# A decoder layer on one core: norm2's sums of late token tiles moved one tile down, four activation splits moved to GpSimd, v transposed instead of multiplied by the identity

## The reference

```
h = rmsnorm(x, norm1_w) * (1 + sc1) + sh1 ;  p = h @ w_in
ya = rmsnorm(a_b * conv3(a_c * a_x)) ;  q, k, v = silu(conv4(qkv))
# DeltaNet, chunk by chunk, state S (128 x 128 per head):
#   v_new = u - w @ S ;  o = q_dec @ S + intra @ v_new ;  S = S * decay + k_dec.T @ v_new
y = concat([ya, rmsnorm(o) * silu(z)]) @ w_out ;  x = x + gt1 * y
h = rmsnorm(x, norm2_w) * (1 + sc2) + sh2
gate, up = split(conv3(h @ w_up)) ;  x = x + gt2 * ((silu(gate) * up) @ w_down)
return rmsnorm(x, norm_f_w)
```

## Time and profile before

| what | us |
|---|---|
| median of 3 runs | 1449.6 (1446.66 to 1451.29) |
| the profiled execution, its own time | 1450.17 |
| its span in the profile | 1447.9 |
| PE busy in the span | 1358.7 (94%) |
| DVE, ACT, POOL busy | 776.0, 554.3, 727.1 |
| mean granted PE clock | 0.966 |

### The profile page before, as it was taken

One profiled execution on the slowest core, in us unless ns is written; L12 is line 12 of the kernel. 1 busy time (PEld: TensorE's weight loads), 2 busy tenths in 40 slices (PEclk: granted clock), 3 DMA queues, 4 the chain that ended last, 5 costly groups with the idle time before them and its releaser, 6 DMA issues.

```text
span 1447.9 us, 18240 instructions
## 1 busy us (share of the span) xinstructions
PE 1358.7 (94%) x6739; PEld 1139.2 (79%) x6739; DVE 776.0 (54%) x959; ACT 554.3 (38%) x749; POOL 727.1 (50%) x488
## 2 busy tenths in 40 slices
PE   3799999999969999989986999999999999999997
PEld 3478888888858999877875888888888877888886
DVE  2834244262446666626465655565556556457544
ACT  3234535262531221215275444444444443324321
POOL 4457758686742212222067655656565565443540
PEclk8699999999969999989998999999999999999999
DMA  8152424224240000110111333322223347443611
GB/s 330 37 131 59 130 72 116 79 81 130 58 132 1 1 0 0 58 59 1 30 30 29 88 87 88 87 81 75 74 78 88 87 156 265 147 138 117 233 36 58
DMA packets 137929, 128.42 MB, mean 89 GB/s; under 512 B 7423, under 2 KB 114188, under 8 KB 137868
## 3 DMA queue, kind: packets, MB, share of 16 engines
q1 hardware_dynamic: 137868, 127.60, 29.1%
HBM read 111.85 MB, written 15.74 MB: 88 GB/s over the span
## 4 chain that ended last, share of the span: by engine, by line
PE 68%; POOL 10%; issue 9%; DVE 7%; DMA 3%; ACT 2%; SPq 0%; POOLq 0%; DVEq 0%; ACTq 0%
PE ps L1930 18%; PE ps L1931 18%; PE ps L1932 18%; PE ps L2060 5%; POOL ada_raw L814 3%; PE ps L2079 3%; PE ps L2076 3%; POOL ada_raw L817 2%; POOL w_split L789 2%; DMA ada_first<-in_ada_w_dram 1%; POOL ada_raw L819 1%; DVE ada_first L1440 1%; DVE pm_b L1584 1%; DMA x_hi<-in_x_dram 1%; POOL ada_sum L823 1%
## 5 line engine op out<-in xcount | busy, mean ns | idle before, releaser
L1930 PE MATMUL ps<-h_p,w_units 128*128 128x512 f32 x616 | 241.2, 392 | 11.7 <-POOL h_p L913 10.2
L1932 PE MATMUL ps<-h_p,w_units 128*128 128x512 f32 x616 | 240.6, 391 | 0.0
L1931 PE MATMUL ps<-h_p,w_units 128*128 128x512 f32 x616 | 240.6, 391 | 0.0
L1930 PE MATMUL ps<-h,w_split 128*128 128x512 f32 x448 | 175.6, 392 | 0.0
L1932 PE MATMUL ps<-h,w_split 128*128 128x512 f32 x448 | 175.1, 391 | 0.0
L1931 PE MATMUL ps<-h,w_split 128*128 128x512 f32 x448 | 175.0, 391 | 0.0
L924 POOL TENSOR_TENSOR w_units<-f_units,w_units 128x512 fp32r<-128x512 f32 x88 | 112.8, 1292 | 114.7 <-ACT w_units L1267 47.6
L949 POOL TENSOR_TENSOR wd_split<-wd_raw,wd_split 128x1024 fp32r<-128x1024 f32 x44 | 109.5, 2494 | 121.2 <-ACT wd_split L1351 121.2
L1881 DVE TENSOR_TENSOR ad_split<-ad_raw,ad_split 128x512 fp32r<-128x512 f32 x44 | 104.3, 2381 | 85.5 <-ACT ad_split L1352 85.4
L1930 PEld LDWEIGHTS ps<-h_p,w_units 128*128 128x128 f32 x616 | 116.3, 189 | 37.1 <-issue 11.0
L1930 PE MATMUL ps<-wd_split,ad_split 128*128 128x512 f32 x352 | 138.1, 392 | 6.0 <-issue 5.7
(11 more groups left out here) (292 smaller groups left out, 2601.3 us busy)
## 6 DMA issues: line engine op xcount, KB each, us to landing
w_up_raw<-in_w_up_dram SPq DMA_DIRECT2D x44, 512.0 KB, 5.4
wd_raw<-in_w_down_dram SPq DMA_DIRECT2D x44, 512.0 KB, 4.2
ada_raw<-in_ada_w_dram SPq DMA_DIRECT2D x32, 512.0 KB, 4.1
w_raw<-in_w_in_dram SPq DMA_DIRECT2D x28, 512.0 KB, 5.4
act_dram<-cg SPq DMA_DIRECT2D x22, 512.0 KB, 3.4
ad_raw<-act_dram SPq DMA_DIRECT2D x44, 256.0 KB, 4.5
ada_first<-in_ada_w_dram SPq DMA_DIRECT2D x4, 2048.0 KB, 17.4
h_room<-in_w_out_dram SPq DMA_DIRECT2D x8, 512.0 KB, 12.9
```

The lines of the kernel that those rows point to most:

```text
L1930: pe.matmul(dst, a_hi, b_hi, start=(first and n == 0), stop=False, skip_group_check=onto)
L1931: pe.matmul(dst, a_hi, b_lo, start=False, stop=False, skip_group_check=onto)
L1932: mm = pe.matmul(dst, a_lo, b_hi, start=False, stop=(last and n == len(pairs) - 1), skip_group_check=onto)
```

## The change

Three edits. (1) In norm2, a late tile's six sums on DVE, its high parts on ACT and its low parts on POOL now stand one tile further down, behind the next tile's statistics; ACT makes the late tile's modulation ahead of the root and the scaling. (2) The low parts of `ad_raw` for the steps 0 to 3 of the down-projection are made by POOL, each behind the weights' low part of the same step; their count moves from `down_act_lo` to `down_lo`, on which SP and PE wait. PE waits for c11, c12, c21 one tile at a time. (3) v is transposed into bank 6.

```diff
+        SPLIT_HERE = 4
+        def down_lo_done(n):
+            return 2 * (n + 1) if n < SPLIT_HERE else n + 1 + SPLIT_HERE
...
@@ gpsimd, down_lo(n)
+                if n < SPLIT_HERE:
+                    pool.wait_ge(s.down_hi, 2 * n + 2)
+                    pool.tensor_tensor(ad_split[slot][:, 1, :], ad_raw[slot][:, :],
+                                       ad_split[slot][:, 0, :].bitcast(F32), ALU.subtract).then_inc(s.down_lo, 1)
-            for n, tt in enumerate(ROWS2[:TT - 1]):
+            def norm2_lo(tt):
                 for op in h_of(tt) if tt < TH else H_LO:
                     h_lo(tt, op)
-                if n == 2:
+            for n in range(1, TT):
+                before = ROWS2[n - 1]
+                if n >= 2 and ROWS2[n - 2] >= TH:
+                    norm2_lo(ROWS2[n - 2])
+                if before < TH:
+                    norm2_lo(before)
+                if n == 3:
                     up_lo(0, 1)
                     up_lo(0, 2)
-                if n == TT - 3:
-                    up_sums_first()
+            up_sums_first()
+            norm2_lo(ROWS2[TT - 2])
             up_lo(0, 3)
@@ scalar
-            for n in range(TT):
-                norm2_rows(n)
-                if n == TT - 1:
-                    keep_p1(0)
-                if n >= 1:
-                    norm2_stage(ROWS2[n - 1])
+            norm2_square(0)
+            norm2_scale(0)
+            for n in range(1, TT):
+                norm2_square(n)
+                before = ROWS2[n - 1]
+                if before >= TH:
+                    norm2_late(before)
+                norm2_scale(n)
+                if n >= 2 and ROWS2[n - 2] >= TH:
+                    norm2_stage(ROWS2[n - 2])
+                if before < TH:
+                    norm2_stage(before)
                 if n == 3:
                     up_top(0, 1)
                     up_top(0, 2)
+            keep_p1(0)
+            norm2_stage(ROWS2[TT - 2])
             up_top(0, 3)
@@ vector
                 inverse_ms(tt, N2 + n + 1)
-                if n >= 1 and ROWS2[n - 1] >= TH:
-                    late_sums(ROWS2[n - 1])
+                if n >= 2 and ROWS2[n - 2] >= TH:
+                    late_sums(ROWS2[n - 2])
+            late_sums(ROWS2[TT - 2])
             norm2_modulate(TT - 1)
             late_sums(TT - 1)
...
@@ vector, the last MLP tile, ahead of take_c12
-                else:
-                    for n in range(3):
-                        down_act_lo(n)
...
-            for n in range(3, STEPS):
+            for n in range(SPLIT_HERE, STEPS):
@@ tensor
                     for hd in range(NH):
-                        pe.matmul(bank(6, 1, P)[:, hd, :], vc[:, hd, :], ident[:, :], start=True, stop=False)
+                        pe.transpose(bank(6, 1, P)[:, hd, :], vc[:, hd, :], ident[:, :])
...
+            down_step(0, range(1))
             pe.wait_ge(s.c11_out, FT)
+            down_step(0, range(1, 2))
             pe.wait_ge(s.c12_out, FT)
+            down_step(0, range(2, 3))
             pe.wait_ge(s.c21_out, FT)
-            down_step(0, range(4))
+            down_step(0, range(3, 4))
             down_step(1, range(4))
```

More of the change, by code:

```diff
@@ L718, in load_down @@
                 else:
-                    sp.wait_ge(s.down_lo, n - RING + 1)
-                    sp.wait_ge(s.down_act_lo, n - RING + 1)
+                    sp.wait_ge(s.down_lo, down_lo_done(n - RING))
+                    if n - RING >= SPLIT_HERE:
+                        sp.wait_ge(s.down_act_lo, n - RING - SPLIT_HERE + 1)
                 sp.dma_start(wd_raw[n % RING][:, :], wdown_v[:, f, :]).then_inc(s.down_in[n % RING], 16)
@@ L1249, in norm2_stage @@
             def norm2_stage(tt):
-                if tt >= TH:
-                    norm2_late(tt)
                 for op in h_of(tt) if tt < TH else H_LATE:
@@ L1268, in up_top, with norm2_square @@
                                ACT.Copy).then_inc(s.up_hi, 1)
-            def norm2_rows(n):
+            def norm2_square(n):
                 tt = ROWS2[n]
@@ L1277, in norm2_rows, with norm2_scale @@
                                accum_out=ss[:, tt:tt + 1]).then_inc(s.norm_ss, 1)
+            def norm2_scale(n):
+                tt = ROWS2[n]
                 wait(s.norm_inv, N2 + n + 1)
@@ L2122, in dn_step @@
                     for hd in range(NH):
-                        pe.matmul(bank(6, 1, P)[:, hd, :], vc[:, hd, :], ident[:, :], start=True, stop=False)
+                        pe.transpose(bank(6, 1, P)[:, hd, :], vc[:, hd, :], ident[:, :])
                         mm = pe.matmul(bank(6, 1, P)[:, hd, :], kg[:, slot, hd, :], st[:, hd, :],
-                                       start=False, stop=True)
+                                       start=False, stop=True, skip_group_check=True)
                     mm.then_inc(s.dn_r, 1)
@@ L2293, in down_tile @@
                 cols = slice(tile % 2 * BANK, (tile % 2 + 1) * BANK)
-                pe.wait_ge(s.down_lo, n + 1)
-                pe.wait_ge(s.down_act_lo, n + 1)
+                pe.wait_ge(s.down_lo, down_lo_done(n))
+                if n >= SPLIT_HERE:
+                    pe.wait_ge(s.down_act_lo, n - SPLIT_HERE + 1)
                 return three_pass(bank(TILE_BANK[tile]), [(ad_split[slot][:, 0, toks], ad_split[slot][:, 1, toks],
```

## The result

The changed kernel takes 1439.3 us (median of 4 runs, 1437.1 to 1442.7) against 1448.7 beside it: ratio 0.9937, 95% interval 0.9919 to 0.9954. Timed again, beside other runs of the kernel before, it came to 0.9924 (0.9905 to 0.9944). So it is faster by 9 to 11 us. The forecast was 4.2 us, and its range ended at 1442.2.

The account below looks back on a forecast made before the run. The prediction took PE to be the bound. Its terms, -1.1 (transposes) + 3.0 (norm2) - 6.1 (border) = -4.2 us, took the profiled 1450.17 to 1446.0, or 1445.4 as a median; range 1442.2 to 1449.0.

Parts of the forecast that it names:

- Border, -6.1: Before the down-projection: pause cut to 1.7 us, 4.1 us gained, and 2.0 more because the clock stays up.
- Rival 1: Before the down-projection the clock falls all the same: gain there 4.1 us, total 1447.4 us; chance 0.2.
- V transposed, -1.1: DeltaNet: PE's row loses 3.8 us in eight chunks, but only the last two chunks give time, 1.1 us.
- Moving them earlier only lengthens the wait: DeltaNet loop: PE's earlier matmuls gain nothing, as the next P product waits for DVE's `um`; six of eight chunks.
- The upper end of 3.8: DeltaNet: the largest gain allowed for the transposes, 3.8 us, all that PE's row loses in eight chunks.
- rival 3: DeltaNet: the transposes bring their 3.8 us in full, sum -6.9, total 1442.7 us; chance 0.07.
- Rival 4: DeltaNet: transposes bring the clock down, up to 2 us in each of eight chunks, total 1461 us; chance 0.05.
- Norm2, +3.0: Norm2 one tile deeper: product 3 starts later and the stage loses 3.0 us; ends 0.6 and 4.5.
- The same spell at half clock follows: Norm2, behind tile 5's turn: the clock falls as before, so the 8.0 us from turn to turn stay.
- the nearest row: Norm2: the old 2.23 us pause before tile 5's turn, which brought the clock down; reason for taking 3.0 us.
- the lower end as given: Norm2: only 0.6 us lost if the clock stays up behind 740 us and in product 1.
- Rival 2: Norm2 costs little or nothing, as the clock stays up behind 740 us: sum about -6.5, total 1443.1; chance 0.15.

Follow-up runs that it names:

- the second profile: The changed kernel with no further edit, profiled again and timed again against the kernel before: ratio 0.9924 (0.9905 to 0.9944).

## Why the prediction was wrong

- **Border, -6.1: right**, in each of its pieces. c12 was free at once, nine matmuls moved ahead, the pause is 1.3 us (1.7 forecast; 0.80 to 2.05 over seven profiles), the clock stays. Alone it gave 6.1 by the ratio, and 5.8 to 7.1 from the last up matmul to the last of all, in the seven profiles that have it. Rival 1 (the clock falls) is out. POOL's four extra splits cost nothing, as said: PE has no other wait from 1100 to 1300 us than the 1.32.
- **V transposed, -1.1: too small by 3 as measured, and by a wrong step.** PE's share (0.105 us a transpose) was right. "Moving them earlier only lengthens the wait" was not: it took the start of `um` as fixed by DVE's row, and never asked what the earlier end of PE's state products releases. It releases POOL's `kg`, which kept DVE waiting 0.28 us in each of the five loop steps behind the first. Five steps give 1.74 us, which the prediction had at nothing; the sixth chunk that it counted, the first step, kept its length. The last two chunks, where the steps leave DVE's row out, gave what was forecast for them: from the seventh chunk's product with v to the output projection it is 31.6 us without the transposes and 30.6 to 30.8 with them in the five profiles with a granted clock of 0.89 there (one without, four with), and 32.9 and 31.8 in the two with 0.84, so 0.9 to 1.1 us. That makes 2.8 us by the schedule. The rest of the 4.1 (2.2 to 5.8) is not shown to be the transposes' work: over all profiles the same stretch is 31.6 to 36.3 us in six without them (mean 34.4) and 29.6 to 33.5 in eight with them (mean 31.3), but it also differs by 2.9 us between two executions of the changed kernel, with a clock of 0.78 in the one and 0.89 in the other. The upper end of 3.8 was taken for PE's own time, so rival 3 had the size, for half the reason. Rival 4 (clock falls in DeltaNet) is out: from the first product with v to the seventh chunk's the clock stayed at full speed.
- **Norm2, +3.0: too large** by 1.5 to 2.4 by the two profiles, and by 2.7 or more by the ratio of norm2 alone. The failed step is "The same spell at half clock follows". The pause was forecast 0.3 us shorter than the old one and came 0.4 shorter; the choice between the ends was made by the nearest row, 2.23 us, and the turn behind 1.82 stayed on the other side. The forecast pause was 1.9 us (737.9 to 739.8), not far from the 1.7 behind which the same prediction let the clock stay at the border. Everything downstream came 1.7 us sooner with it: POOL's row began 21.2 us behind the turn of tile 2, not 22.9. POOL's row itself was right: 21.3 us from its first low part to product 3 in the second profile (748.06 to 769.35), as worked out. Product 3 ended up 0.6 us later than before by that profile, which is the lower end as given. Rival 2 is the case that came in.
- **Sum.** With 0.6 for norm2 and 2.8 for the transposes the same working gives 8.3; with the 4.1 that the transposes measured alone it gives 9.6. The whole measured 9 to 11, so 1 to 3 us are left that no step of the working names; half-clock spells differ by that much from run to run, but which ones it was is open. The two errors had the same sign, and the range had counted them as alternatives, each with its own small chance, instead of letting them add.

## What to carry to other kernels

When two engines' chains end at the same moment, shortening one gives nothing and shortening both gives all: before calling an edit hidden, look at what its earlier end releases, on every engine, and whether that work shares a port with the chain that hides it. Where GpSimd and VectorE run side by side, compare one VectorE instruction's duration with and without company; a few tenths of a microsecond there can be the loop's length. And of a pause that an edit shortens by a little, ask on which side of the clock's fall it ends: here 0.57 us more of pause put the next turn 2.1 us back. Near that border read more than one profile: the same 2.23 us kept the clock in one kernel and lost it in seven others.

## What the runs showed of the hardware

- Before the turn of tile 5 the clock stayed at 2.4 GHz behind a pause of 1.79 to 1.82 us (five profiles). It fell to 1.2 GHz behind 2.23 to 2.25 us in seven of eight profiles, and behind 2.37 (one). At the border it stayed behind 0.80 to 2.05 us (seven profiles) and fell behind 3.65, and behind 2.16 that came 1.0 us after another of 0.38.
- GpSimd's 1.28 us multiply held up a 0.43 us VectorE instruction to 0.71, 0.87 and 1.52, always to 0.27 to 0.29 us past its own end. VectorE's split with two inputs in SBUF took 0.68 us with nothing beside it and 2.48 and 2.87 beside GpSimd's weight splits (the two in 5.27).
- Four fp32 transposes of 128x128 in each chunk, mixed one by one with products, left the granted clock at 1.00 from the first chunk's to the seventh's.
